# A decoder step with 32 experts: down weights loaded in another row order, gate and up read at a stride of four

## What is computed

```python
def hier_moe(x, w_group_router, w_expert_router, w_gate, w_up, w_down):
    ...
    eid = (g_sel[:, None] * EXPERTS_PER_GROUP + top_e).reshape(-1)
    tok = jnp.repeat(jnp.arange(N), TOP_K_EXPERTS)
    order = jnp.argsort(eid)
    tok_s = tok[order]
    sizes = jnp.bincount(eid, length=N_EXPERTS).astype(jnp.int32)
    xs = x[tok_s]
    hid = jax.nn.silu(lax.ragged_dot(xs, w_gate, sizes)) * lax.ragged_dot(xs, w_up, sizes)
    ys = lax.ragged_dot(hid, w_down, sizes) * wts[order][:, None].astype(x.dtype)
    return jax.ops.segment_sum(ys, tok_s, num_segments=N)
```

## Time and profile before

| what | value |
|---|---|
| median of three runs | 1577.37 us |
| lowest, highest | 1575.47, 1581.02 us |
| profiled execution, its time | 1579.47 us |
| its span (first to last instruction) | 1577.6 us |
| mean granted TensorE clock | 0.951 |
| PE busy | 1420.0 us (90%) |
| L1854, gate and up, PE busy | 429.7 us |
| L1863, down, PE busy | 220.7 us |
| DMA over the span | 385.29 MB, mean 244 GB/s |

### The profile page before, as it was taken

How to read it: one execution, slowest core, us unless ns; L and a number is a source line. 1 busy time by engine, 2 the same in 40 slices (tenths; PEclk the granted TensorE clock), 3 DMA queues, 4 the chain that set the end, 5 groups by cost and what they waited for, 6 DMA issues and landing times. The chain is left out here.

```text
span 1577.6 us, 24986 instructions
## 1 busy us (share of the span) xinstructions
PE 1420.0 (90%) x9447; PEld 676.1 (43%) x9447; DVE 574.1 (36%) x1273; ACT 365.1 (23%) x809; POOL 323.3 (20%) x494
## 2 busy tenths in 40 slices
PE   5989988899999899996299999999999999999954
PEld 2644444444556544553244444444444444444421
DVE  1246999960355367436710111011101111111128
ACT  1334555311566421010011111111111111000014
POOL 0217444596100024321000000000000000000036
PEclk8999999999899999987599999999999999999977
DMA  8717222221121254312869999999999999999745
GB/s 330 288 32 256 67 65 82 72 76 60 36 78 33 81 151 161 130 58 98 325 241 379 389 405 399 408 409 404 399 409 407 403 399 407 401 395 389 303 158 185
DMA packets 98559, 385.29 MB, mean 244 GB/s; under 512 B 19808, under 2 KB 37280, under 8 KB 85181
## 3 DMA queue, kind: packets, MB, share of 16 engines
q1 hardware_dynamic: 75228, 327.54, 53.8%
q10 hardware_dynamic: 16384, 32.52, 6.1%
q0 software_dynamic: 6880, 24.38, 5.0%
HBM read 344.39 MB, written 40.00 MB: 244 GB/s over the span
## 5 line engine op out<-in xcount | busy, mean ns | idle before, releaser
L1854 PE MATMUL psum<-wgu,xgT 128*32 128x256 f32 (+1 forms) x3840 | 429.7, 454 | 10.7 <-DVE xgT L2026 9.3
L1854 PEld LDWEIGHTS psum<-wgu,xgT 128*32 128x32 f32 (+1 forms) x3840 | 173.1, 119 | 262.7 <-issue 203.4
L678 PE MATMUL psum<-w_sb,mixT 128*128 128x512 f32 x512 | 230.1, 603 | 13.6 <-ACT u L873 7.9
L1863 PE MATMUL psum<-wd,hidT 128*32 128x256 f32 (+1 forms) x1920 | 220.7, 454 | 0.0
L678 PEld LDWEIGHTS psum<-w_sb,mixT 128*128 128x128 f32 x512 | 95.9, 192 | 137.0 <-issue 112.1
L1905 POOL DMA_INDIRECT xg<-h_dram,tokens x32 | 29.5, 922 | 531.2 <-PE psum L1846 483.4
L1863 PEld LDWEIGHTS psum<-wd,hidT 128*32 128x32 f32 (+1 forms) x1920 | 79.9, 119 | 127.1 <-issue 100.9
L2032 DVE TENSOR_TENSOR hid<-silu,psum 128x256 f32<-128x256 f32 x40 | 16.9, 422 | 286.2 <-ACT silu L1973 286.2
L1434 PE MATMUL psum<-w_o,mixT 128*128 128x512 f32 x256 | 114.7, 608 | 1.1 <-PEq L1165 1.1
L980 DVE TENSOR_SCALAR_CACHE_REDUCE above<-bias,cand 128x384 int8<-128x384 f32 (+3 forms) x128 | 108.2, 846 | 4.5
L1973 ACT ACTIVATE silu<-psum 128x256 f32<-128x256 f32 x40 | 15.3, 383 | 348.1 <-PE psum L1854 348.1
(11 more groups left out here) (365 smaller groups left out, 1593.4 us busy)
## 6 DMA issues: line engine op xcount, KB each, us to landing
wgu<-in_w_gate_dram SPq DMA_DIRECT2D x40, 2048.0 KB, 17.1
wgu<-in_w_up_dram SPq DMA_DIRECT2D x40, 2048.0 KB, 22.0
wd<-in_w_down_dram SPq DMA_DIRECT2D x40, 2048.0 KB, 22.5
ada_b<-in_w_ada_dram ACTq DMA_DIRECT2D x16, 1024.0 KB, 5.0
ys_dram<-yy ACTq DMA_DIRECT2D x80, 128.0 KB, 8.5
ys_dram<-zero SPq DMA_DIRECT2D x22, 384.0 KB, 5.1
ada_a<-in_w_ada_dram SPq DMA_DIRECT2D x4, 2048.0 KB, 15.3
w_sb<-in_w_in_dram SPq DMA_DIRECT2D x4, 2048.0 KB, 10.2
```

The lines of the kernel that those rows point to most:

```text
L678: last = nc.tensor.matmul(bank[2 + n % 2], mixT[:, k, t * P:(t + 1) * P], w_sb[:, k, n0:n0 + 512], start=(k == 0), stop=(k == DC - 1))
L1854: last = nc.tensor.matmul(out[m * j:m * j + m, 0:2 * w], xgT[:, b, k, first:first + m], wgu[:, b, :, k, w * j:w * j + w], start=(k == 0), ...
L1863: last = nc.tensor.matmul(out[m * j:m * j + m, 0:w], hT(k), wd[:, b, k, w * j:w * j + w], start=(k == 0), stop=(k == KD - 1))
```

## The change

The view of the down weights is cut the other way: partition p now gets rows 4p to 4p+3, which lie together in HBM, 16 KB. The hidden unit on partition p of block k is then 4p+k in place of 128k+p. So that `hid` comes out of `gate_up` in this order, the moving operand is read as `(c q)`: for each residue q all columns c*4+q, c from 0 to 127. Half j takes the residues 2j and 2j+1, quarter j the residue j. The loads on SP change from 128x4x1024 to 128x4096 elements; the number and the order of the instructions on each engine stay as they were. One line is added in `gate_up`, so later lines of the program move down by one (L1854 becomes L1855, L1863 becomes L1864).

```diff
-        wd_v = a["w_down"][0].rearrange("e (k p) n -> e p k n", k=KD)
+        wd_v = a["w_down"][0].rearrange("e (p k) n -> e p k n", k=KD)
...
             def gate_up(b, out, m, first, n):
 
-                w = DE // n
+                w, q = DE // n, KD // n
                 for k in range(DC):
+                    both = wgu[:, b, :, k, :].rearrange("p g (c q) -> p g q c", q=KD)
                     for j in range(n):
-                        last = nc.tensor.matmul(out[m * j:m * j + m, 0:2 * w], xgT[:, b, k, first:first + m], wgu[:, b, :, k, w * j:w * j + w],
+                        last = nc.tensor.matmul(out[m * j:m * j + m, 0:2 * w], xgT[:, b, k, first:first + m], both[:, :, q * j:q * j + q, :],
                                                 start=(k == 0), stop=(k == DC - 1))
                 return last
```

## The result

The changed kernel takes **2026.76 us** (median of four runs, 2023.47 to 2029.04), the kernel before 1576.42 us beside it (four runs, 1575.39 to 1581.02). The ratio is 1.2852, with a 95% interval of 1.2822 to 1.2883: 450 us slower, where no change was forecast.

What follows compares the result with a forecast made beforehand. PE was taken to set the pace, with DMA just keeping up. 1579.47 us profiled - 0.6 (down loads) + 0 (strided gate and up) = 1578.9, or 1576.8 us against the runs; range 1570 to 1640 us, chance 0.80.

Steps and rivals of the forecast that it cites:

- PE sets the pace, not the load: Expert stage: PE works without a gap, 17.40 us per expert, and waits only 0.6 us in all for weights.
- I take 0: Gate and up's strided moving columns: price taken as 0, between ends of 0 and +303 us.
- the first row: Transposes of L1846 on PE: weight loads at a 32-byte stride, 0.109 us each, read as showing no loss.
- The upper end: Gate and up: 1.7 times as much per strided element, as on VectorE, would add 303 us to 432.4 us.
- VectorE's row: VectorE reduction of 288 elements at a 32-byte stride (L1695): 0.66 us against 0.45 together, 1.74 ns per strided element.
- Rival 1: All MATMULs of gate and up: strided moving operand is slower, 1880 us at 1.7 times, 2009 at twice; chance 0.12.
- Rival 2: Gate and up: side-by-side streams hinder each other, 1626 to 2302 us; large form 0.08, part of it in small loss's 0.13.
- rivals 3 and 4: 3: load bounds, 1569 us (0.05 with any gain); 4: down stays in 4 KB packets, within 0.6 us (in 0.62).
- The down loads: SP's queue: 384 packets fewer per expert, worth 0 to -0.6 us in the whole kernel; -0.6 taken.
- the question whether large packets of down could delay others: Loads and gathers sharing the DMA engines: delay from down's large packets taken as 0.

## Why the prediction was wrong, point by point

- **PE sets the pace, not the load: right.** PE's longer stage became the kernel's loss nearly one to one (449.8 us in two rows, 446.2 between the two profiled executions), and the DMA share fell to 0.60 with nothing gained or lost by it.
- **"I take 0, because the first row is on PE and at its own pace, while VectorE's has another clock": this is the step that failed.** The row on PE was of a transpose's weight load, and that is the one kind of read in these runs that takes such a stride almost for free (0.109 and 0.118 us per load); the same engine's ordinary weight loads (0.232) and its moving operands (0.913 against 0.447 us a step) pay. The row on another engine was the right neighbour.
- **The upper end was mis-sized as well.** I turned VectorE's row into a factor, 1.7, against its own pace of 1.02 ns. Its absolute price, 1.74 ns per element, carries over: 12288 columns * 40 tiles * 1.74 ns = 855 us for gate and up, where 882 were measured. As a bound that is 1577 + 855 - 432 = 2000 us, against 2026.76. The other clock, which I held against the row, did not matter: the price came out alike on both engines, and on PE it did not follow the granted clock.
- **Rival 1 is what happened**, in its form "twice", 2009 us, to which I gave no part of the range: the chance of 0.12 lay in what 1570 to 1640 left out. The sign that I had named for it, both shapes growing by one factor, came out (2.04 and 2.03).
- **Rival 2 falls**: one stream pays as much as two or four. So do rivals 3 and 4: the new rows of down alone made nothing faster, and their packets did go from four to one per partition.
- **The down loads: -0.6 us expected, a loss of 0.1% to 0.5% measured alone.** The packets changed as forecast, but the 0 that I gave to the question whether large packets of down could delay others was wrong: PE waited 5.2 us more for up. In the changed kernel nothing of it shows.
- **The rule of the Trainium skill** that spoke against the change (SBUF — State Buffer, section "Door 1: The DMA port swizzle": at least two hits on a 16-byte line) deserved more than a share of rival 1: one row of two agreed with it, and the other was of an operand that the change does not touch.

## What to carry to other kernels

Count the 16-byte pieces that a strided operand touches and price them in nanoseconds, not as a factor: here 1.72 to 1.76 ns each on PE's moving operand, against 0.84 ns per fp32 column of the array, and 1.74 and 1.75 ns for each strided element on VectorE. So two columns in a piece are nearly free, and four in an aligned run quite. A row on the same engine is no price for an operand of another kind (moving, stationary, in a transpose): here VectorE's row came nearer than that of PE's transposes. Where the trace has none, a run with one line strided settles it. A transfer that already keeps up buys nothing by a better row, above all when the other side of the reordering falls on the engine that sets the pace.

## What the runs showed of the hardware that was not expected

- A strided read costs nearly the same on two engines: 1.72 and 1.76 ns per new aligned 16 bytes on PE's moving operand (from the strides of two, three and four), and on VectorE, where pieces were not told from elements, 1.75 and 1.74 ns per element at strides of 16 and 32 bytes. On PE it does not change with the granted clock (22.02 us for the first tile, begun at 0.50, 21.98 for the next at 1.00; sixteen strided loads of L1388 in 3.81 us at either level).
- The loads of a transpose take a stride of 16 or 32 bytes at 0.118 and 0.109 us per 128 columns; at the same strides the loads of an ordinary fp32 matmul go from 0.110 to 0.232 and 0.237.
- Sixteen KB in one packet where there were four of 4 KB did not load faster: 392 to 400 GB/s at a share of 1.01, against 403 to 405 at 1.02.
